# Expert weights of a two-layer MoE: two experts read before the routing is known, the table of units kept on chip

## What is computed

```python
def hier_moe(h, wgc, bgc, wgf, bgf, w1, w3, w2):
    ...
    pg = jax.nn.softmax(jnp.dot(t, wgc, preferred_element_type=f32) + bgc.astype(f32), axis=-1)
    gw, gi = lax.top_k(pg, 1)
    ...
    tv, ti = lax.top_k(jax.nn.softmax(fs, axis=-1), TOP_K_IN_GROUP)
    ...
    gates = jnp.sum(jax.nn.one_hot(eid, N_EXPERTS, dtype=f32) * wts[..., None], axis=1)
    a = jnp.einsum('td,edf->tef', t, w1)
    c = jnp.einsum('td,edf->tef', t, w3)
    act = jax.nn.silu(a) * c * gates[:, :, None].astype(t.dtype)
    y = jnp.einsum('tef,efd->td', act, w2)
    return y.reshape(B, S, D)

def second_block(...):
    ...
    for i in range(DEPTH):
        ...
        h = layer_norm(DN_ALPHA * h + mix, ln1_g[i], ln1_b[i])
        y_moe = hier_moe(h, ...)
        y_ple = jax.nn.sigmoid(h @ ple_wg[i] + ple_bg[i]) * (p[i] @ ple_wp[i])
        h = layer_norm(DN_ALPHA * h + y_moe + y_ple, ln2_g[i], ln2_b[i])
```

## Time and profile before

| | us |
|---|---|
| median of 3 runs (3307.08 to 3312.53) | 3311.17 |
| the profiled execution | 3306.85 |
| its span | 3305.0 |
| expert stage of the first layer, TensorE's first to last step | 2473.6 to 2643.3 |
| expert stage of the second layer | 3088.6 to 3249.1 |
| TensorE busy | 3047.3 (92%) |

### The profile page before, as it was taken

How to read it: one execution, slowest core, us unless ns; L and a number is a source line. 1 busy time by engine, 2 the same in 40 slices (tenths; PEclk the granted TensorE clock), 3 DMA queues, 4 the chain that set the end, 5 groups by cost and what they waited for, 6 DMA issues and landing times.

```text
span 3305.0 us, 40644 instructions
## 1 busy us (share of the span) xinstructions
PE 3047.3 (92%) x15776; PEld 2191.2 (66%) x15776; DVE 1531.0 (46%) x2270; ACT 1133.5 (34%) x1786; POOL 1227.8 (37%) x734
## 2 busy tenths in 40 slices
PE   6899988999999999999989999899878979998786
PEld 4666656888888778687768888574562268466324
DVE  5655546552331533323251112556665544667554
ACT  4244325211111422222252222434325633434463
POOL 3343333454443425233255555362430035444001
PEclk9699989999999999999999999999999989999898
DMA  5200121444331112121133333121259542133893
GB/s 208 100 28 26 64 71 63 160 153 144 124 109 64 52 50 78 45 71 61 42 107 102 96 96 96 53 64 57 78 207 423 211 145 77 32 97 92 332 404 110
DMA packets 89350, 379.35 MB, mean 115 GB/s; under 512 B 9798, under 2 KB 14408, under 8 KB 80072
## 3 DMA queue, kind: packets, MB, share of 16 engines
q1 hardware_dynamic: 71880, 314.61, 26.9%
q10 hardware_dynamic: 12672, 45.37, 3.5%
q0 software_dynamic: 4608, 16.78, 1.5%
HBM read 542.39 MB, written 29.36 MB: 173 GB/s over the span
## 4 chain that ended last, share of the span: by engine, by line
PE 74%; DVE 12%; ACT 4%; DMA 4%; SPq 3%; issue 2%; POOL 1%; DVEq 0%; ACTq 0%; POOLq 0%
PE PS L105 73%; DVE SCR L117 2%; DVE SCR L129 2%; DMA ALL<-in_moe 2%; DVE SCR L123 2%; ACT SCR L111 1%; ACT RT L111 1%; DVE XF L123 1%; PE PS L108 1%; SPq L164 1%; DVE BF L129 1%; SPq L156 1%; SPq L147 1%; ACT WH L111 1%; DVE SM L132 1%
## 5 line engine op out<-in xcount | busy, mean ns | idle before, releaser
L105 PE MATMUL PS<-RT,WH 128*128 128x512 f32 (+1 forms) x5728 | 1539.3, 371 | 64.6 <-DVE RT L123 26.6
L105 PEld LDWEIGHTS PS<-RT,WH 128*128 128x128 f32 x5728 | 1039.6, 191 | 308.2 <-issue 54.7
L117 POOL TENSOR_TENSOR WL<-RAW,WH 128x1024 fp32r<-128x1024 f32 x286 | 704.8, 2467 | 858.7 <-ACT WH L111 858.6
L105 PE MATMUL PS<-RT,WL 128*128 128x512 f32 (+1 forms) x2864 | 934.8, 367 | 0.0
L105 PEld LDWEIGHTS PS<-RT,WL 128*128 128x128 f32 x2864 | 497.9, 192 | 58.2
L111 ACT ACTIVATE WH<-RAW 128x1024 fp32r<-128x1024 f32 x286 | 301.0, 1055 | 625.1 <-PE PS L105 580.9
L117 POOL TENSOR_TENSOR RT<-SCR,RT 128x512 fp32r<-128x512 f32 (+2 forms) x174 | 231.2, 1335 | 459.1 <-ACT RT L111 316.7
L105 PE MATMUL PS<-ALL,SCR 128*32 x576 | 272.4, 618 | 60.1 <-DVE RTX L114 33.2
L117 DVE TENSOR_TENSOR SCR<-PS,SCR 128x512 f32<-128x512 f32 (+1 forms) x106 | 58.8, 572 | 486.7 <-PE PS L105 476.5
L105 PE MATMUL PS<-RTX,SCR 128*32 128x512 f32 x1152 | 272.5, 625 | 0.0
L105 PE MATMUL PS<-BF 128*128 128x512 f32 (+2 forms) x612 | 259.8, 604 | 5.8 <-DVE SCR L117 4.4
(11 more groups left out here) (194 smaller groups left out, 3531.6 us busy)
## 6 DMA issues: line engine op xcount, KB each, us to landing
ALL<-in_moe SPq DMA_DIRECT2D x94, 2048.0 KB
ALL<-in_moe SPq DMA_DIRECT2D x94, 1024.0 KB
RAW<-in_ff SPq DMA_DIRECT2D x132, 512.0 KB, 3.4
BF<-in_ada SPq DMA_DIRECT2D x64, 512.0 KB, 4.3
RAW<-in_ret SPq DMA_DIRECT2D x64, 512.0 KB, 3.2
RTX<-in_ada SPq DMA_DIRECT2D x32, 512.0 KB, 4.4
RAW<-in_win SPq DMA_DIRECT2D x28, 512.0 KB, 3.5
XF<-placed_in ACTq DMA_DIRECT2D x24, 512.0 KB, 9.2
```

What stands on the lines that cost most here:

```text
L105: return NOTHING if self.e is None else self.e.matmul(o, w, x, start=first, stop=last)
L117: return NOTHING if self.e is None else self.e.tensor_tensor(*a)
```

## The change

The first two experts by number (0 and 1, `FIRST`) now always take the first two places, whether they have rows or not, and are read by four unconditional loads that `sp_first_experts` issues ahead of the fourth of ple's ten weight loads. The conditional loads of the others begin after the scatter, and the other three places are handed out in the order in which they come free: 24576, 39680, 6144; the last two no longer have a wait of SyncE for themselves but two more counts in `in_free` and `out_free`, which VectorE gives by tiny memsets ("w" and "h"). Expert and "new" are packed into one number (16 * new + expert), and the count to wait for is kept in its register for the out part. The table is turned by three small matmuls of TensorE against the identity and copied to EXR and EXA by VectorE; the four small DMAs and the tile EXT are gone. `dve_gates` moves from the end of the routing into the expert stage, behind the copies of step 2 of block 2.

```diff
-PLACES = (14336, 31400, 39680, 6144, 24576)
+PLACES = (14336, 31400, 24576, 39680, 6144)
+FIRST = 2
...
@@ pe_route
             pe_embed(pe, i, 4)
+            o = take_bank(pe, ("un", i))
+            pe.wait_ge(*dve_done.at(("un", i)))
+            for c in range(3):
+                t = pe.matmul(o[0:1, 4 * NQ * c:4 * NQ * c + 4 * NQ], VALUES[:, c:c + 1], IDT[:, 0:4 * NQ], True, True)
+            t.then_inc(*pe_done.done(("un", i)))
...
@@ dve_route
+            dve.scalar_tensor_tensor(VALUES[:, 2:3], found[:, 1:2], 4.0, held[:, 0:1], ALU.is_ge, ALU.add).then_inc(
+                *dve_done.done(("un", i)))
             dve_embed(dve, i, 4)
+            turned = bank.of(("un", i))[0:1, 0:12 * NQ]
+            dve.wait_ge(*pe_done.at(("un", i)))
+            dve.tensor_copy(EXR.rearrange("p (j c) -> p c j", c=3), turned.rearrange("p (c j) -> p c j", c=3)).then_inc(
+                *dve_done.done())
+            dve.tensor_copy(EXA, turned[:, 4 * NQ:8 * NQ]).then_inc(*dve_done.done(("route", i)))
...
+            dve.wait_ge(*pe_done.at(("ep", i, 7, 0)))
+            dve.memset(found[:, 0:1], 0.0).then_inc(*in_free.done(("w", i)))
+            dve.memset(found[:, 1:2], 0.0).then_inc(*out_free.done(("w", i)))
             dve_embed(dve, i, 7)
-            dve_gates(dve, i)
+            dve.wait_ge(*dve_done.at(("x", ("ln2", i), 7)))
+            dve.memset(found[:, 0:1], 0.0).then_inc(*in_free.done(("h", i)))
+            dve.memset(found[:, 1:2], 0.0).then_inc(*out_free.done(("h", i)))
...
@@ sp_experts
+            def load(j, z):
+                a, size, sem = ((0, 4096, in_free), (4096, 2048, out_free))[z]
+                if not z:
+                    c = 3 * (j % 4 * NQ + j // 4)
+                    unit[j] = (*sp.registers(f"unit{i}_{j}_", EXR[:, c:c + 2], 2, (31, max(PLACES))),
+                               sp.value_load(EXR[:, c + 2:c + 3], 1, 2 * NQ + 6))
+                row, to, free = unit[j]
+                sp.wait_count(sem.sem, free)
+                sp.dma_if(row // 16, ALL[:, bass.ds(to + a, size)], io[f"moe{i}"][bass.ds(row % 16, 1), :, a:a + size].rearrange(
+                    "a p f -> (a p) f")).then_inc(*unit_in[j // 4][z].done((i, j // 4, z), by=16))
...
             sp.wait_ge(*dve_done.at(("route", i)))
-            sp.dma_start(ED, EXT[0:4 * NQ, :]).then_inc(*table_in.done(by=16))
...
+            sp.wait_ge(*first_in.at(("first", i)))
+            sp.wait_ge(*placed.at(("sc", i)))
...
+        def sp_first_experts(sp, i):
             sp.wait_ge(*pe_done.at(("wo", i, 7, 0)))
...
+            for a, size in ((0, 4096), (4096, 2048)):
+                for e in range(FIRST):
+                    sp.dma_start(ALL[:, PLACES[e] + a:PLACES[e] + a + size], io[f"moe{i}"][e, :, a:a + size]).then_inc(
+                        *first_in.done(("first", i), by=16))
...
@@ dve_experts
                 dve_copy(dve, i, n, u)
+                if (n, u) == (2, 2):
+                    dve_gates(dve, i)
...
@@ sp_program
+                if name.startswith("ple") and i == 3:
+                    sp_first_experts(sp, int(name[3:]))
                 load_unit(sp, u)
```

More of the change, by code:

```diff
@@ L2977, in sp_experts @@
-            sp.wait_ge(*table_in.at(("table", i)))
-            sp.wait_ge(*pe_done.at(("wo", i, 7, 0)))
-            unit = {}
[L2981 to L2985, removed]
-                    if j == 3 and not z:
-                        sp.wait_ge(*dve_done.at(("x", ("ln2", i), 7)))
-                    if j == 4 and not z:
-                        sp.wait_ge(*placed.at(("sc", i)))
-                    c = 4 * (j % 4 * NQ + n)
-                    if not z:
-                        unit[j] = sp.registers(f"unit{i}_{j}_", EXR[:, c:c + 3], 3, (15, max(PLACES), 1))
-                    row, to, new = unit[j]
-                    free = sp.value_load(EXR[:, c + 3:c + 4], 1, 2 * NQ + 2)
-                    sp.wait_count(sem.sem, free)
-                    sp.dma_if(new, ALL[:, bass.ds(to + a, size)], io[f"moe{i}"][bass.ds(row, 1), :, a:a + size].rearrange(
-                        "a p f -> (a p) f")).then_inc(*unit_in[n][z].done((i, n, z), by=16))
@@ L2999, in sp_experts @@
-            load(0, 0)
-            for n in range(NQ):
-                if n + 1 < NQ:
-                    load(n + 1, 0)
-                load(n, 1)
+            unit = {}
+            def load(j, z):
[8 more added lines that the diff above has]
+                    "a p f -> (a p) f")).then_inc(*unit_in[j // 4][z].done((i, j // 4, z), by=16))
@@ new lines, in units @@
+            def units(n):
+                return range(4 * n, min(4 * n + 4, NUNIT))
+            sp.wait_ge(*dve_done.at(("route", i)))
+            sp.wait_ge(*first_in.at(("first", i)))
+            sp.wait_ge(*placed.at(("sc", i)))
+            for j in units(0):
+                load(j, 0)
+            for n in range(NQ):
+                for j in units(n + 1):
+                    load(j, 0)
+                for j in units(n):
+                    load(j, 1)
+        def sp_first_experts(sp, i):
+            sp.wait_ge(*pe_done.at(("wo", i, 7, 0)))
+            for a, size in ((0, 4096), (4096, 2048)):
+                for e in range(FIRST):
+                    sp.dma_start(ALL[:, PLACES[e] + a:PLACES[e] + a + size], io[f"moe{i}"][e, :, a:a + size]).then_inc(
+                        *first_in.done(("first", i), by=16))
@@ L3013, in wait_copy @@
         def wait_copy(eng, i, n, u):
+            if (n, u) == (0, 0):
+                eng.wait_ge(*first_in.at(("first", i)))
             if u in (0, 4):
@@ L3031, in pe_step @@
         def pe_step(pe, i, n, u, outs, x, first, last, events):
+            if (n, u) == (0, 0):
+                pe.wait_ge(*first_in.at(("first", i)))
             if u in (0, 4):
```

41 lines of the change are left out of this document (22 added, 19 removed).

## The result

The changed kernel takes 3279.3 us (median of 5 runs, 3272.9 to 3285.6), the kernel before 3311.2 on the same chip (5 runs): ratio 0.9913, 95% interval 0.9891 to 0.9935, so some 29 us less by the ratio and 32 by the medians. The prediction was 3289, 22 us less, in a range of 3277 to 3302: right in sign and inside its range, 7 to 10 us short in size.

The account below looks back on a forecast made before the run. TensorE's work fills most of the span; its expert-stage waits were put down to DMA loads, delayed by bandwidth and late issue. -10.5 - 12.5 + 2 x 0.5 = -22.0 us gave 3284.9, as median 3289, range 3277 to 3302.

Parts of the forecast that it names:

- Block 0 of the first layer, 9.1 us earlier: First expert step, experts 0 and 1 long there: TensorE starts at 2464.5, 9.1 us earlier, a 4 us wait staying.
- Block 1, 7 us earlier: First layer: expert 3, issued by the walk at 2463.6, lets TensorE start at 2476.8 against 2483.80; 7 us left.
- The cover of the early loads: Ple's fourth load, behind the early loads, lands near 2385, 22 us before ScalarE's split at 2406.93; costs nothing.
- The table, 0.5 us a layer: Routing: three TensorE matmuls turning the table cost 0.5 us a layer; the removed round trips, hidden before, gain nothing.
- The queue of loads decides up to block 7: First layer: 4.2 MB less to move after 2460, 10.1 us; waits at blocks 1, 4, 7; layer -10.5 us.
- (A): Rival, only the starts count: later waits are for free places, not bytes; about -12 us, 3299; chance 0.16.
- Walk: SyncE's conditional loads: in part 1.87 us, out part about 0.5, four units 9.5 instead of 11.7; start no earlier.
- Second layer, -12.5: Second expert stage: block 0 starts 6.1 us earlier, block 8's wait goes (11.3), a new 4.9 before block 9.
- Gates: VectorE's 1.65 us moved to block 2's copies: at most about 1.3 us a layer, absorbed by later waits; counted nothing.
- B: Rival, all bytes count: 15 us in the first layer, 17.5 in the second, 3280; chance 0.12.
- C: Rival, slower: SyncE's walk becomes the bound above 3.1 us a unit; at 3.4, 3317; chance 0.05.
- D: Rival: early loads' cover too thin, delaying ple's fourth load past ScalarE's split, or start gains nothing; 3309; chance 0.07.

Follow-up runs that it names:

- early_only: Kernel before with only the early loads of experts 0 and 1 added, all else as before: 3305.3 us, ratio 0.9993.
- walk_reloads: Changed kernel, but out parts of SyncE's walk read their count from the table again instead of keeping it: 3282.5 us, ratio 0.9918.
- static_waits: Changed kernel, but SyncE again waits at unit 2 for the last projection and at unit 3 for VectorE's last sum: 3286.3 us, ratio 0.9943.
- no_early: Changed kernel without its early loads, all 16 experts conditional and read by the walk: 3283.8 us, ratio 0.9929.
- gates_back: Changed kernel with dve_gates back at the end of the routing: 3274.7 us, ratio 0.9895; again on another chip 3268.9 us, ratio 0.9890.
- casts_ahead: Changed kernel with gates at the routing's end and VectorE's casts of the table ahead of its embedding part 4: 3274.2 us, ratio 0.9902.
- walk_early: Changed kernel with gates at the routing's end, casts ahead of part 4 and SyncE's walk not waiting for the scatter: 3277.0 us, ratio 0.9901.
- old_places: Changed kernel with the old order of places (39680, 6144, 24576) and counts to match: 3280.9 us, ratio 0.9917.

## Why the prediction was right, and where not

**Block 0 of the first layer, 9.1 us earlier: right.** The wait fell from 13.15 to 4.91, 8.2 us; 4 us were to stay, 4.9 stayed. **Block 1, 7 us earlier: about right.** Against the start of the first wait its first step comes 8.7 us earlier (14.7 us behind it, 23.4 before), and no wait is left at it, where one was forecast; the 0.81 stands before its third step.

**The cover of the early loads: right.** ScalarE's split of ple's fourth unit is at 2409.06, with no wait; 2406.93 plus the 2.1 us by which this profile was late at ple's first load already.

**The table, 0.5 us a layer: right, but not all that was added there.** By early_only, walk_reloads and static_waits the first layer loses 0.5 us ahead of its stage. That nothing else would move by more than 1 us did not hold: 2.4 us at the lower clock came on top in the changed kernel.

**"The queue of loads decides up to block 7", 4.2 MB for 10.1 us: the step that failed.** Its result, -10.5, came out as -14.0 in waits (29.0 to 15.0) and -16.4 from the start of the first wait to the stage's end. But the reason is another. With the bytes alone out (early_only) the first layer wins 6 us, less than its block 0 does, and the kernel nothing. With the early loads taken back (no_early), where two thirds of their bytes fall outside the full stretch, it loses 3 us of waits. In the chain of the changed kernel the load ahead of a late block goes when TensorE is through with a block and SyncE has walked on from there, and then stands 14 to 19 us in a full queue. That loop is shortened by a block 0 that starts early and by a SyncE that is there when the place comes free. SyncE's waits for TensorE's counts at the loads of its first walk (total us, times, longest, from 2449 to 2650 us, first of the changed kernel and then of the one before) tell the same: in the changed kernel it stands ready and waits for places, in the kernel before far less.

```profile
SPq L148 <- PE PS L106: 24.1, 7, 6.9
```

```profile
SPq L147 <- PE PS L105: 6.9, 3, 4.8
```

I had named this rival (A) and put it at 0.16 and -12, since I took the starts for all that it could leave. The sign that I had given for it, an idle DMA while TensorE waits, shows in early_only and not in the changed kernel (share 0.96 from 2460 to 2594): a full DMA does not speak against a loop of places. The loads ahead of blocks 4 and 7:

```profile
2506.18 14.07 DMA ALL<-in_moe
...
2543.21 19.21 DMA ALL<-in_moe
```

**The two waits by number.** I had them in the walk's times (expert 3 at 2463.6 and not 2470.3) but in no term of their own. They are the largest: 11 us of waits, and 9 to 12 us of time by the ratios, which come from different groups of runs.

**Walk: the costs right, the start not.** In parts were to cost 1.87 us and cost 1.72 to 1.79, out parts 0.5 and 0.46. I saw no gain in the start, and took the scatter for what sets it; it is set by VectorE's casts, 0.2 us behind the scatter, and against the last indirect store it is 1.7 us earlier (8.6 us after it before, 6.9 now). The rule on `tensor_load` that I cited from the Trainium skill ("DMA: Bandwidth & Descriptors", Latency and other measured facts), some 600 ns at least, does not hold in these traces: 0.27 us for one word and 0.47 for two.

**Second layer, -12.5: right to 1 us by the profile** (-13.5 by the stage's end), by other shares. Its first wait fell by 8.7 instead of 6.1 us, block 8's went, and the new one before block 9 is 3.1 instead of 4.9. That no wait stands at block 8 needs the cheap out parts (walk_reloads brings 7.62 us back), and the first wait needs the order of places and the early loads (15.35 and 14.87 us without them).

**Gates: counted as nothing, for a reason that was not tested.** I let later waits take up 1.65 us inside the stage. At the old place the gates cost nothing either (first wait 4.92), so moving them gained nothing; whether it lost 5 us, as the medians of gates_back would have it, or 1 or less, as the profiles would, is open.

**Rivals.** B (all bytes count) gave 3280, nearest to the result, by a reason that early_only refutes: a time that fits proves no mechanism. C and D did not occur: SyncE's walk of the first layer is 24 us shorter, and ScalarE's split of ple's fourth unit was not delayed.

**The total.** The forecast was short mostly in the first layer: -16.4 there instead of -10.5, less the 3.0 us that its routing lost. That it came near and inside the range is in part luck, since the first layer's figure rested on bytes.

Undone one at a time, early loads, waits by number, cheap out parts and order of places cost 8, 11, 6 and 7 us of waits in single profiles; that is more than the 26.7 that the whole change saves, so the parts' shares overlap and cannot be added. No run puts the table's DMAs back. The lowest times of the study are those of gates_back, 0.9895 and 0.9890 on two chips against 0.9906 to 0.9916 for the change, with intervals that overlap.

## What to carry to other kernels

Ask of a queue that walks through conditional work which item each wait was meant for, and tie it to that item: here a wait tied to a position held everything behind it. Where buffers are freed by the consumer, bytes taken out of a full stretch need not be time: what counts is whether the loop of free, load, land and use is shorter. Test by undoing and by doing alone, since a part of a change may be worth nothing singly, as the early loads here. Compare windows of two traces from a common event, not by their absolute times: the same step came up to 17 us apart here. Before removing a wait, look for a second one that ends at the same moment.

## What the runs showed of the hardware

- Loads of registers cost by the word: 0.27 us for one, 0.47 for two, 0.68 for three on SyncE; on VectorE its 24 words take 1.74 us and run beside its earlier vector work.
- From GpSimd's last indirect store to the walk's first issue lie 6.75 us where the scatter sets it (casts_ahead) and 4.7 where SyncE does not wait for it (walk_early). The 6.9 of the changed kernel are set by VectorE's casts.
- One core's DMA ran at 397 to 415 GB/s over the full stretch of 134 us.
- The profile and the medians of 6 runs disagree by up to 7 us for walk_reloads and old_places. Runs of one kernel spread over 5 to 20 us, so parts of this size are better read from the waits, which three profiles of the changed kernel give within 1.3 us; a cost in time is then not shown.
